# VectorE's order at the end of a stage: additions to the residual, and the rests of the next stage's first two pieces

## The chip, the cores and the metric

The kernel runs on one core of a Trainium2 chip. The core has the engines TensorE (PE, matmuls), VectorE (DVE), ScalarE (ACT), GpSimd (POOL) and SyncE (SP, here only a DMA queue). Each takes its instructions in order; they wait for one another through semaphores. The metric is the device time of one execution in microseconds (us). The kernel before takes 2769.25 us, the median of three runs (2766.05 to 2773.75).

## The reference

A block of two layers and a second block of two layers work on 256 tokens of 1024 channels in float32:

```
# first block, per layer l = 0, 1
h = rmsnorm(x, norm1_g[l]);  x = x + token_mixer(h, w_in[l], ..., w_out[l])      # mix1
h = rmsnorm(x, norm2_g[l])
x = x + swiglu(h, gate, up, down)        # l = 0: ffn1, width 3584
x = x + moe_ffn(h, router, 8 experts)    # l = 1: moe, top 2 of 8, width 3584 each
x = rmsnorm(x, final_g)                                                          # post
# second block, per layer l = 0, 1
x = x + 0.5 * swiglu(rms_norm(x, ffn1_norm), ...)                                # ffn2a, width 2816
x = x + concat(attention, conv) @ w_out  # of rms_norm(x, mix_norm)              # mix2
x = x + 0.5 * swiglu(rms_norm(x, ffn2_norm), ...)                                # ffn2b, width 2816
x = rms_norm(x, post_norm)                                                       # post
```

with `rmsnorm(x, g) = x * rsqrt(mean(x * x) + 1e-6) * g` and `swiglu(h) = (silu(h @ gate) * (h @ up)) @ down`.

## The kernel before

**Stages.** `plan` (line 69) lists the stages in order: mix1, ffn1, mix1, moe, post, and then twice ffn2a, mix2, ffn2b, post. A post stage is only the closing norm. `after(st)` gives the next stage that is no post stage.

**Pieces.** All weights come in pieces of 128 x 2048 float32 (1 MB; a few of mix2 are smaller). SP loads them in order into a ring of six slots, `raw`. To keep the precision of float32, a piece is split in two: ScalarE rounds it into `hi` (`act_hi`, line 439; a ring of three slots), and VectorE subtracts that from the piece, which leaves the rest, `lo` (`lo_piece`, line 1185; it overwrites `raw`). Activations are split in the same way into `xh` and `xl` (in a feed-forward stage's hidden part `hh` and `hl`). Each product is then three matmuls: high by high, high by rest, rest by high. The semaphores `hi_done`, `lo_done` and `multiplied` count pieces. A load into a slot of `raw` waits for `multiplied` of the piece six before, a rounding for that of the piece three before.

**Stage end.** The last four pieces of a mixer and every third of a feed-forward stage multiply into four PSUM banks of 128 x 512, which hold the stage's result for two halves of 128 tokens. For the last piece `pe_last_rows` (lines 737 to 749) does all of the first token half before the second. It raises `first_tile` behind the first half and `multiplied` behind the second. VectorE's `add_down` (line 1252) then adds the four banks to the residual `x` (line 1261), two for each half, and raises `x_done` behind each half. The expert stage (moe) has no `add_down`: it adds within `experts` and then calls `ahead` itself (line 1691).

**Ahead.** The first two pieces of the next stage are split before that stage's norm: ScalarE rounds them in `act_ahead` (line 479), and VectorE makes their rests in `ahead` (line 1222). The second of them is rounded only when the piece before the last is multiplied, since its slot of `hi` is taken until then.

**Norm.** Behind `act_ahead`, ScalarE squares and sums the two halves of `x`, each when `x_done` says so (line 493). VectorE's `norm` (line 1227) makes of each sum a variance (`var`, line 1232), ScalarE takes the root (line 497), and VectorE makes the reciprocal (line 1237) and scales `x` by it and by the gain into `xn` (line 1244; in a post stage into `x`, line 1239). In program order VectorE has both var instructions first, and then reciprocal and scaling for each half. TensorE transposes `xn` into PSUM (line 1071), ScalarE rounds the result into `xh` (line 510), VectorE makes `xl` (line 1249), and the next stage's matmuls begin. POOL loads the gain of a norm when the squares of the norm before it are done (line 1110).

Of the kernel before, what the change touches and what calls it, by code (L numbers as in the profile page):

```python
# [96 lines left out]
def build(nc, A, rope, out):  # L97
    stages = plan()

    with ExitStack() as ctx:  # L100
# [216 lines left out]
        def after(st):  # L317

            return next((n for n in stages[st["Q"] + 1:] if n["kind"] != "post"), None)
# [841 lines left out]
        def _(dve):  # L1161
# [21 lines left out]
            def lo_piece(S, c, i, n=PIECE):  # L1183
                dve.wait_ge(S.hi_done, c + 1 + 6 * i)
                v.tensor_tensor(lo[:, c % RING, 0:n], raw[:, c % RING, 0:n], hi[:, c % HRING, 0:n].bitcast(F32),  # L1185
                                ALU.subtract).then_inc(S.lo_done, 1)
# [35 lines left out]
            def ahead(st):  # L1222

                lo_piece(main, st["B"], 0)
                lo_piece(main, st["B"] + 1, 0)
# [25 lines left out]

            def add_down(st, factor, end):

                if after(st):
                    ahead(after(st))
                dve.wait_ge(first_tile, st["W"] + 1)
                for b in range(4):
                    if b == 2:
                        dve.wait_ge(main.multiplied, end)
                    xs = x[:, b // 2, b % 2 * 512:b % 2 * 512 + 512]  # L1260
                    ins = v.scalar_tensor_tensor(xs, bank[DOWN[b]][:, :], factor, xs, ALU.mult, ALU.add)
                    if b % 2:
                        ins.then_inc(x_done, 1)

            def turned_rest(dst, src, gain, high, signal):

                v.scalar_tensor_tensor(dst, src, gain, high.bitcast(F32), ALU.mult, ALU.subtract).then_inc(signal, 1)  # L1267

            def mix1(st):
# [91 lines left out]
                for k in range(KD):  # L1361
                    dve.wait_ge(ev("yh_out"), 8 * l + bank_end(k, KD))
                    turned_rest(xl[:, k, :], bank[Y_BANKS[k // 2]][:, k % 2 * T:(k % 2 + 1) * T],
                                col(("group", l), k), xh[:, k, :], ev("yl_out"))
                lo_piece(main, B + 11, 0)
                add_down(st, 1.0, B + MIX1_PIECES)

            def router(st):
# [124 lines left out]
            def mix2(st):  # L1493
# [139 lines left out]
                for b in range(2):  # L1633
# [6 lines left out]
                                ALU.subtract).then_inc(ev("catl_out"), 1)  # L1640
                lo_piece(main, B + 13, 0)
                add_down(st, 1.0, B + MIX2_PIECES)

            def constants():
# [27 lines left out]
            for st in stages:  # L1672
                k = st["kind"]
                norm(st)
                if k == "post":
                    continue
                if st["M"] == 0:
                    constants()
                if k == "mix1":
                    mix1(st)  # L1680
                elif k == "mix2":
                    mix2(st)
                elif k == "moe":
                    router(st)
                    experts(main, st, 0)
                    flag = dve.value_load(spill[0:1, 0:1])
                    with dve.If(flag > 0):
                        experts(again, SPILL, 1)
                        dve.nop()
                    dve.end_ifs()  # L1690
                    ahead(after(st))
                    mark(x_done, TT)
                else:
                    ffn(st)
                    add_down(st, 1.0 if k == "ffn1" else 0.5, st["B"] + 3 * st["n"])
# [67 lines left out]
```

## Time and profile before

| | |
|---|---|
| median of three runs | 2769.25 us (2766.05 to 2773.75) |
| profiled execution | 2773.95 us, its span 2771.9 us |
| busy: TensorE, VectorE, ScalarE, POOL | 2482.3, 1796.3, 1381.2, 26.5 us |
| mean granted clock of TensorE | 0.941 of full speed |
| read from HBM | 596.94 MB, 216 GB/s over the span |
| one subtraction of line 1185 | 2.28 us on average, 562 of them |

The profiled execution took 2.05 us around its span. Busy times are sums over a program whose stages differ, so what a change is worth is read where it acts: at the ends of stages. A matmul's start is measured, its end is modelled. In the timelines a merged row gives the start of the first instruction, the busy time of all of them, and in brackets how long the engine sat idle before and what ended that.

### The profile page before, as it was taken

How to read it: one execution, taken by the hardware profiler on the slowest of the kernel's cores; microseconds unless marked ns; L12 is line 12 of the kernel's file. 1: busy time of each engine (PE TensorE's matmuls, PEld its weight loads, DVE VectorE, ACT ScalarE, POOL GpSimd, SP SyncE). 2: the span in 40 equal slices, each digit the busy share in tenths (PEclk: the TensorE clock that was granted, in tenths of full speed). 3: DMA queues.
4: the chain of work that ended last, by engine and by line, in shares of the span. 5: the costliest groups of instructions: out<-in, count | busy, mean ns of one | idle time of the engine just before them, and what ended most of it. 6: DMA issues, size and time to landing. Idle time of an engine off the chain costs nothing.

```text
span 2771.9 us, 42658 instructions
## 1 busy us (share of the span) xinstructions
PE 2482.3 (90%) x16893; PEld 2310.4 (83%) x16893; DVE 1796.3 (65%) x1813; ACT 1381.2 (50%) x1297; POOL 26.5 (1%) x50
## 2 busy tenths in 40 slices
PE   5799987999999999999999799865899899846998
PEld 5699986898989899989989699864799799835897
DVE  5544456588888888787888744559444544486544
ACT  3443334476767666676767544341444433432433
POOL 2000000000000000000000000000000000000000
PEclk9899999799999999999999899985899999976999
DMA  6345543498989898899989645430355455411452
GB/s 222 124 168 189 188 157 131 172 361 310 361 310 360 309 346 323 327 335 331 338 317 354 248 168 186 163 124 1 129 183 187 154 189 182 141 61 46 161 188 98
DMA packets 84816, 599.06 MB, mean 216 GB/s; under 512 B 9812, under 2 KB 10038, under 8 KB 13574
## 3 DMA queue, kind: packets, MB, share of 16 engines
q1 hardware_dynamic: 81216, 587.76, 59.2%
q0 software_dynamic: 3040, 9.13, 1.0%
q8 instruction: 52, 0.85, 0.1%
q10 hardware_dynamic: 486, 1.13, 0.1%
q14 instruction: 22, 0.18, 0.0%
HBM read 596.94 MB, written 1.05 MB: 216 GB/s over the span
## 4 chain that ended last, share of the span: by engine, by line
PE 83%; DVE 12%; ACT 3%; issue 1%; DMA 1%; ACTq 0%; DVEq 0%
PE bank L718 9%; PE bank L720 9%; PE bank L719 9%; PE bank L732 9%; PE bank L733 9%; PE bank L734 9%; PE bank L761 8%; PE bank L763 8%; PE bank L767 8%; DVE lo L1185 3%; DVE acc L1541 3%; ACT hi L439 1%; PE bank L845 1%; PE bank L1071 1%; DMA stage_rows<-in_sgu_b 1%
## 5 line engine op out<-in xcount | busy, mean ns | idle before, releaser
L1185 DVE TENSOR_TENSOR lo<-raw,hi 128x2048 fp32r<-128x2048 f32 (+1 forms) x562 | 1276.9, 2280 | 727.4 <-ACT hi L439 726.3
L439 ACT CAST hi<-raw 128x2048 fp32r<-128x2048 f32 (+1 forms) x562 | 1064.4, 1899 | 642.0 <-PE bank L767 322.1
L732 PE MATMUL bank<-hi,xh 128*128 128x256 f32 (+2 forms) x2088 | 610.0, 292 | 30.4 <-DVE xl L1267 12.8
L733 PE MATMUL bank<-lo,xh 128*128 128x256 f32 (+2 forms) x2088 | 599.0, 287 | 0.0
L734 PE MATMUL bank<-hi,xl 128*128 128x256 f32 (+2 forms) x2088 | 598.7, 287 | 0.0
L718 PE MATMUL bank<-xh,hi 128*128 128x256 f32 x2080 | 591.7, 284 | 7.0 <-DVE xl L1249 7.0
L719 PE MATMUL bank<-xl,hi 128*128 128x256 f32 x2080 | 591.0, 284 | 0.0
L720 PE MATMUL bank<-xh,lo 128*128 128x256 f32 x2080 | 590.9, 284 | 0.0
L732 PEld LDWEIGHTS bank<-hi,xh 128*128 128x128 f32 x2088 | 404.7, 194 | 45.7 <-issue 18.8
L718 PEld LDWEIGHTS bank<-xh,hi 128*128 128x128 f32 x2080 | 401.7, 193 | 11.0 <-DVE xl L1249 8.9
L733 PEld LDWEIGHTS bank<-lo,xh 128*128 128x128 f32 x2088 | 405.5, 194 | 3.2
L734 PEld LDWEIGHTS bank<-hi,xl 128*128 128x128 f32 x2088 | 404.8, 194 | 0.6
L719 PEld LDWEIGHTS bank<-xl,hi 128*128 128x128 f32 x2080 | 401.8, 193 | 2.1
L720 PEld LDWEIGHTS bank<-xh,lo 128*128 128x128 f32 x2080 | 401.6, 193 | 0.0
L761 PE MATMUL bank<-hi,hh 128*128 128x512 f32 x872 | 342.7, 393 | 12.2 <-DVE hl L1202 12.2
L763 PE MATMUL bank<-lo,hh 128*128 128x512 f32 x872 | 342.3, 393 | 0.0
L767 PE MATMUL bank<-hi,hl 128*128 128x512 f32 x872 | 269.7, 390 | 0.0
L446 ACT ACTIVATE sg<-bank 128x256 f32<-128x256 f32 (+1 forms) x170 | 78.2, 460 | 253.3 <-PE bank L720 222.0
L761 PEld LDWEIGHTS bank<-hi,hh 128*128 128x128 f32 x872 | 164.8, 189 | 45.9 <-issue 8.6
L767 PEld LDWEIGHTS bank<-hi,hl 128*128 128x128 f32 x872 | 164.1, 188 | 35.5
L763 PEld LDWEIGHTS bank<-lo,hh 128*128 128x128 f32 x872 | 164.8, 189 | 29.2
L1197 DVE TENSOR_TENSOR hf<-sg,bank 128x256 f32<-128x256 f32 (+1 forms) x170 | 86.2, 507 | 102.6 <-PE bank L720 91.1
(268 smaller groups left out, 1576.9 us busy)
## 6 DMA issues: line engine op xcount, KB each, us to landing
raw<-in_moe_w_gate SPq DMA_DIRECT2D x112, 1024.0 KB, 4.9
raw<-in_moe_w_up SPq DMA_DIRECT2D x112, 1024.0 KB, 4.9
raw<-in_moe_w_down SPq DMA_DIRECT2D x112, 1024.0 KB, 4.9
raw<-in_ffn_w_gate SPq DMA_DIRECT2D x58, 1024.0 KB, 4.9
raw<-in_ffn_w_up SPq DMA_DIRECT2D x58, 1024.0 KB, 4.9
raw<-in_ffn_w_down SPq DMA_DIRECT2D x58, 1024.0 KB, 4.9
raw<-in_mix_pieces SPq DMA_DIRECT2D x46, 1024.0 KB, 4.9
gains<-in_norm_g POOLq DMA_DIRECT2D x4, 512.0 KB, 7.3
```

Source lines behind the costliest of these rows:

```text
L439: nc.scalar.copy(hi[:, c % HRING, 0:n], raw[:, c % RING, 0:n]).then_inc(S.hi_done, 1)
L718: pe.matmul(o, hi[:, hr, a:a + P], xh[:, k, 0:w], start=(k == 0), stop=False)
L719: pe.matmul(o, hi[:, hr, a:a + P], xl[:, k, 0:w], start=False, stop=False)
L720: mm = pe.matmul(o, lo[:, r, a:a + P], xh[:, k, 0:w], start=False, stop=(k == KD - 1))
L732: pe.matmul(o, xh[:, x0 + k, tk], hi[:, hr, wgt], start=(first and n == 0), stop=False)
L733: pe.matmul(o, xh[:, x0 + k, tk], lo[:, r, wgt], start=False, stop=False)
L734: mm = pe.matmul(o, xl[:, x0 + k, tk], hi[:, hr, wgt], start=False, stop=(last and n == len(ks) - 1))
L761: pe.matmul(o, ah[:, s, tk], hi[:, hr, wgt], start=(first and s == 0), stop=False, skip_group_check=True)
L763: pe.matmul(o, ah[:, s, tk], lo[:, r, wgt], start=False, stop=False, skip_group_check=True)
L767: mm = pe.matmul(o, al[:, s, tk], hi[:, hr, wgt], start=False, stop=(last and s == 1), skip_group_check=True)
L1185: v.tensor_tensor(lo[:, c % RING, 0:n], raw[:, c % RING, 0:n], hi[:, c % HRING, 0:n].bitcast(F32), ALU.subtract).then_inc(S.lo_done, 1)
L1197: v.tensor_tensor(o, a, b, ALU.mult).then_inc(S.hf_done, 1)
```

## The change

In `add_down` the two lines that call `ahead` move from the front to the end. VectorE makes the four additions first and the rests of the next stage's first two pieces behind them. Nothing else differs. At the end of the last stage `after(st)` is empty and the function is as before.

```diff
             def add_down(st, factor, end):
 
-                if after(st):
-                    ahead(after(st))
                 dve.wait_ge(first_tile, st["W"] + 1)
                 for b in range(4):
                     if b == 2:
                         dve.wait_ge(main.multiplied, end)
                     xs = x[:, b // 2, b % 2 * 512:b % 2 * 512 + 512]
                     ins = v.scalar_tensor_tensor(xs, bank[DOWN[b]][:, :], factor, xs, ALU.mult, ALU.add)
                     if b % 2:
                         ins.then_inc(x_done, 1)
+                if after(st):
+                    ahead(after(st))
```

## Rows read from the trace of the kernel before

**Rows 1.** Page, part 4: the chain that ended last, by engine.

```profile
PE 83%; DVE 12%; ACT 3%; issue 1%; DMA 1%; ACTq 0%; DVEq 0%
```

**Rows 2.** Waits of SP's queue, whole trace: us in total, times, longest.

```profile
SPq L356 <- PE bank L747: 46.8, 8, 6.8
```

**Rows 3.** Line 1261, the additions: count and duration in ns.

```profile
L1261 DVE SCALAR_TENSOR_TENSOR x<-bank,x x36: 677/680/692, 125.4 to 2763.9; 128x512 f32<-128x512 f32 x36
```

**Rows 4.** Chain of waits, end of ffn1: start us, us, what.

```profile
372.57 4.49 DVE lo L1185 x2
377.06 2.40 DVE x L1261 x4
...
381.03 0.76 DVE xn L1244
```

**Rows 5.** DVE's timeline, end of ffn1: start us, us, instruction [idle before].

```profile
376.99 2.47 DVE L1261 SCALAR_TENSOR_TENSOR x<-bank,x 128x512 f32<-128x512 f32 x4
```

**Rows 6.** DVE's timeline, end of the first mixer.

```profile
117.75 2.29 DVE L1185 TENSOR_TENSOR lo<-raw,hi 128x2048 fp32r<-128x2048 f32 x1 [3.15 <-ACT hi L439]
...
125.40 2.52 DVE L1261 SCALAR_TENSOR_TENSOR x<-bank,x 128x512 f32<-128x512 f32 x4
...
129.50 1.42 DVE L1244 SCALAR_TENSOR_TENSOR xn<-x,rstd,gains 128x512 f32<-128x512 f32 x2
```

**Rows 7.** DVE's timeline, the last stage, which has none after it.

```profile
2760.60 1.29 DVE L1261 SCALAR_TENSOR_TENSOR x<-bank,x 128x512 f32<-128x512 f32 x2 [3.11 <-PE bank L747]
2763.32 1.29 DVE L1261 SCALAR_TENSOR_TENSOR x<-bank,x 128x512 f32<-128x512 f32 x2 [1.43 <-PE bank L747]
2764.52 0.14 DVE L1232 TENSOR_SCALAR var<-ssq 128x1 f32<-128x1 f32 x1
2765.82 0.15 DVE L1232 TENSOR_SCALAR var<-ssq 128x1 f32<-128x1 f32 x1 [1.15 <-ACT xn L493]
```

**Rows 8.** PE's timeline, end of ffn1: last piece, transposes.

```profile
371.52 0.73 PE L747 MATMUL bank<-hi,hh 128*128 128x512 f32 x2 [1.43 <-DVE hl L1202]
...
381.84 3.67 PE L1071 MATMUL bank<-ident,xn 128*128 128x128 f32 x16 [4.59 <-DVE xn L1244]
```

**Rows 9.** PE's timeline, end of the first mixer: last piece, transposes.

```profile
121.00 0.61 PE L747 MATMUL bank<-hi,xh 128*128 128x512 f32 x2
...
130.30 1.32 PE L1071 MATMUL bank<-ident,xn 128*128 128x128 f32 x8 [3.71 <-DVE xn L1244]
```

**Rows 10.** PE's timeline, the last stage: last piece's first matmuls.

```profile
2757.55 0.73 PE L747 MATMUL bank<-hi,hh 128*128 128x512 f32 x2 [1.43 <-DVE hl L1202]
```

**Rows 11.** DVE's timeline inside a mixer: a root fetched from ScalarE.

```profile
1939.94 0.17 DVE L1626 TENSOR_SCALAR var<-bna 128x2 f32<-128x2 f32 x1
1940.38 0.17 DVE L1628 RECIPROCAL rstd<-std 128x2 f32<-128x2 f32 x1 [0.27 <-ACT std L649]
1940.58 1.53 DVE L1630 TENSOR_SCALAR xn<-bank,bna,rstd 128x512 f32<-128x512 f32 x2
```

**Rows 12.** Windows, PE, the 6 us after a seam: busy, PEclk, DMA.

```profile
485.10:491.10 6.00, 6.00 (x36) 0.63 0.01 3
1589.80:1595.80 6.00, 6.00 (x28) 0.50 0.00 0
1791.70:1797.70 6.00, 6.00 (x50) 1.00 0.00 0
...
2183.50:2189.50 6.00, 5.97 (x39) 0.75 0.00 0
```

**Rows 13.** Waits, all engines: the only one of a conversion on weights.

```profile
ACT hi L439 <- DMA raw<-in_mix_pieces: 4.9, 2, 3.7
```

**Rows 14.** POOL's timeline at the seam with a closing norm.

```profile
2173.29 0.53 POOL L1110 DMA_DIRECT2D gains<-in_ffn_norm  x1 [198.69 <-ACT xn L493]
```

**Rows 15.** Tile gains at that seam: landing times.

```profile
DMA to landing us min/median/max: 3.9/3.9/3.9
```

**Rows 16.** Chain of waits at that seam.

```profile
2177.64 0.76 DVE xn L1244
```

## The prediction

> **What bounds the kernel now.** I read first the shares of the chain that ended last: TensorE has 83% of it and VectorE 12% [rows 1]. So the kernel is bound by matmuls, with stretches between stages in which VectorE sets the time. Then I looked for transfers, because a time bound by them could swallow a delay. There are none: SP's queue stands waiting for TensorE to release a slot, at each of the 8 last pieces that have a stage after them too [rows 2], and of all conversions of weights only two waited for a transfer, 4.9 us together [rows 13].
>
> The additions of line 1261 are 36, four for each of nine stages [rows 3]. One of the nine, the last, has no stage after it. So the change acts at 8 places, which I call seams: four end a feed-forward stage (ffn1, ffn2a twice, the first ffn2b), four end a mixer. The expert stage makes its two rests by a path of its own and is not touched.
>
> The chain at a seam shows that the two rests (lo) and the four additions stand on the path one behind the other, and that behind them come the squares, the root and the scaling that feeds the transposes [rows 4]. At a mixer's end only the second rest stands in front of the additions; the first was made 7.6 us earlier in idle time of VectorE [rows 6].
>
> **The change, part by part.** It adds and removes no instruction, transfer or semaphore. Per seam two 128x2048 subtractions move from before the four additions to behind them, and so ahead of the two var instructions, the reciprocals and the scaling of the next norm, which VectorE takes in order.
>
> *What it takes off.* The last stage is a feed-forward stage without these rests and shows when the additions can start. Its last piece starts on TensorE at 2757.55 [rows 10], the first pair of additions starts at 2760.60 (3.05 later), the second at 2763.32 (5.77), and the next instruction runs at 2764.52 (6.97) [rows 7]. At ffn1's end the piece starts at 371.52 [rows 8] and the additions run from 376.99 for 2.47 us, to 7.94 after it [rows 5]. So the additions end 0.97 us earlier. At the mixer's end the piece starts at 121.00 [rows 9]. Its first pair of matmuls took 0.61 us against 0.73 [rows 8, 9], so I take 0.12 off: the additions would end 6.85 after it, where they end now at 125.40 + 2.52 = 127.92, or 6.92 [rows 6]. There the gain is 0.07, since TensorE's last matmul, not the rest, all but sets their end already.
>
> *What it puts on.* The two rests take 376.99 - 372.57 = 4.42 us, from the first's start to the additions' [rows 4, 5]. Behind the additions the squares of the second half run on ScalarE anyway; the wait for them covers part of this. In the last stage the var instruction that needs them starts at 2765.82, or 8.27 after the piece's start [rows 7, 10]. The rests end at 6.97 + 4.42 = 11.39 (mixer 11.27). So the squares are hidden and the rests are what is late. Then the root has to be fetched from ScalarE: now the first half's root is ready while the second half's squares run, in the changed kernel both var instructions come only behind the rests. The same fetch inside a mixer takes 1940.58 - 1939.94 = 0.64 us from var to the first use [rows 11].
>
> *The sum per seam*, as the start of the scaling (xn) after the last piece's start:
> - feed-forward: now 381.03 - 371.52 = 9.51 [rows 4, 8]; then 11.39 + 0.64 = 12.03; later by 2.52.
> - mixer: now 129.50 - 121.00 = 8.50 [rows 6, 9]; then 11.27 + 0.64 = 11.91; later by 3.41.
>
> Four of each: 10.1 + 13.6 = 23.7 us. From the scaling on, transposes, rounding and the first matmuls are the same instructions, so all of it moves. What lies ready is the rest that the next stage's first matmul wants: it ends 0.64 us ahead of the scaling.
>
> *Queues that the step is moved past.* ScalarE waits for VectorE meanwhile and its two roundings of weights are ahead of the squares as before. SP's queue waits for TensorE alone. POOL loads a gain when the squares are done. At the seam with a closing norm this is close now: issued at 2173.29, 3.9 us to land, first used at 2177.64 [rows 14 to 16], a slack of 0.45. Afterwards the use is 2.5 us later and the squares end no later. Now the issue goes out beside the closing norm's first reciprocal, 4.35 before the use. In the changed kernel that reciprocal comes 0.44 behind the rests' end (1940.38 - 1939.94 [rows 11]) and the use some 4.35 behind it, 4.8 in all. So even if the issue could not go out beside VectorE's rests and waited for their end, it would land 3.9 after it, in time. I take 0; the bounds are 0 and 0.5.
>
> *The clock of TensorE.* Its idle time before the transposes, now 4.59 (feed-forward) and 3.71 (mixer) [rows 8, 9], becomes about 7.1 at both (4.59 + 2.52, 3.71 + 3.41). In the 6 us after a seam's first matmul the granted clock is not the same at all of them: at three of the eight it is 1.00 (the first at 1791.7), at five between 0.63 (485.1) and 0.75 (2183.5) [rows 12]. With two levels, 2.4 and 1.2 GHz, the time lost in 6 us is 6 x (1 - clock): 0 at three, about 1.9 at five, 9.4 in all. The longer idle time cannot be read from any seam exactly; the nearest ones are the eight themselves, with gaps of 3.7 and 4.6, and the expert stage's seam, idle far longer, with 0.50, or 3.0 lost [rows 12]. I take half of what the three full-clock seams could lose, 3 x 1.9 / 2 = +3. Bounds: -9.4, all seams at full clock, and 8 x 3.0 - 9.4 = +14.6.
>
> The Trainium skill's page "TensorE: Matmul & The Clock Gate", section "Part 1: The HAM clock gate (the "warmup" mystery)", says that an idle TensorE falls to half clock and gets the full one back only after sustained activity. The trace agrees in part: by that rule no seam with this much idle time should find the full clock at its first matmuls, and three do, their transposes having run just before. Its result is the second rival.
>
> Together 23.7 + 3 = 26.7 us. Set on the profiled execution's 2773.95 this is 2800.7. That execution is 4.7 us above the median of the three runs, 2769.25; the difference applies to either, and a median is what will be compared, so 2769.25 + 26.7 = 2796.
>
> **The rivals.**
> 1. *Every seam starts at the low clock.* The three seams at 1.00 lose as the five do: 3 x 1.9 = 5.7, or 2.4 to 3.0 at each if they behave as the expert stage's. For it: the idle time grows by 2.5 to 3.4 us. Against it: the idle time is not all that decides, since both clocks are found behind today's gaps. 23.7 + 5.7 to 14.6, some 33 us: 2802.
> 2. *The clock falls out kindly.* The delayed starts land so that more seams find the full clock; the five lose half: -4.7, so +19: 2788.
> 3. *Not slower: transfers are the bound behind the seams and catch up.* If a stage later waits for its weights, 3 us of delay at its start let the transfers run ahead and the wait shrinks by the same amount. This decides from the point where such waits sum to the 23.7 us put on. Against it: 4.9 us of them in the whole trace, and a ring of pieces that is full, so that SP can't run ahead [rows 2, 13]. With all absorbed and the 0.97 of four seams kept it would be 2769 - 4 = 2765.
> 4. *The change does less than it says*: the rests are hidden in the wait for squares wholly. Then the additions' earlier end would remain. It would need rests of 8.27 - 6.97 = 1.30 us, a third of what is measured; I give it no more than a trace of chance, with rival 3.
>
> **How the numbers follow.** Forecast (24 to 30 us more) 0.62, rival 1 0.20, rival 2 0.14, rivals 3 and 4 0.04. The predicted time is the forecast's, 2796. The range goes from 2785 (+16, most of rival 2) to 2806 (+37, rival 1 with its longer low stretches). Runs of the kernel before lie between 2766.05 and 2773.75, which the ends allow for too. About 0.3%, 8 us, can be told from no change. Faster 0.01, same 0.03, slower 0.96: only rivals 3 and 4, or a very kind clock, stay below 8 us.
>
> **What would show it.** In the profile of the changed kernel: the first pair of additions waits for TensorE, 3.05 us (feed-forward) or 2.9 (mixer) after its last piece's start; the second pair starts 2.7 later; directly behind it the two rests with no idle time, and then two var instructions side by side; the scaling starts 12.0 and 11.9 after the last piece's start; TensorE's idle time before the transposes is near 7.1 at seven seams and longer only at the one with a closing norm. I am wrong if a rest is found before the additions, if the scaling shifts by other amounts, if SP's waits for TensorE vanish behind a seam, or if the sum of the eight shifts is right but the time is not: then it is the clock term.

## The result and the profile after

The changed kernel took 2789.9 us, the median of three runs (2789.6 to 2791.34), against 2769.25: 20.65 us more, a ratio of 1.0075 (95% interval 1.0055 to 1.0095). Five more rounds gave 1.0087 (1.0073 to 1.0100). Its profiled execution took 2789.6 us, its span 2787.6.

The chain by engine is nearly the same as [rows 1]:

```profile
PE 84%; DVE 12%; ACT 2%; issue 1%; DMA 1%; ACTq 0%; DVEq 0%
```

VectorE's timeline at ffn1's end, the answer to [rows 4, 5] (start us, us, instruction, idle time before):

```profile
373.06 1.29 DVE L1259 SCALAR_TENSOR_TENSOR x<-bank,x 128x512 f32<-128x512 f32 x2 [3.11 <-PE bank L747]
375.77 1.29 DVE L1259 SCALAR_TENSOR_TENSOR x<-bank,x 128x512 f32<-128x512 f32 x2 [1.43 <-PE bank L747]
376.98 4.48 DVE L1185 TENSOR_TENSOR lo<-raw,hi 128x2048 fp32r<-128x2048 f32 x2
381.38 0.20 DVE L1232 TENSOR_SCALAR var<-ssq 128x1 f32<-128x1 f32 x2
381.86 0.16 DVE L1237 RECIPROCAL rstd<-std 128x1 f32<-128x1 f32 x1 [0.28 <-ACT std L497]
382.06 1.42 DVE L1244 SCALAR_TENSOR_TENSOR xn<-x,rstd,gains 128x512 f32<-128x512 f32 x2
```

The additions now wait for TensorE in two pairs, and behind them the two rests run without a gap. The last piece started at 370.00, so the scaling at 382.06 is 12.06 behind it; it was 9.51, and 12.03 was forecast. The two var instructions stand side by side behind the rests, and the reciprocal waits 0.28 for the root: var to scaling is 0.68, forecast 0.64.

The same at the first mixer's end, for [rows 6]:

```profile
120.28 1.29 DVE L1259 SCALAR_TENSOR_TENSOR x<-bank,x 128x512 f32<-128x512 f32 x2 [9.31 <-PE bank L747]
123.00 1.29 DVE L1259 SCALAR_TENSOR_TENSOR x<-bank,x 128x512 f32<-128x512 f32 x2 [1.43 <-PE bank L747]
124.20 4.48 DVE L1185 TENSOR_TENSOR lo<-raw,hi 128x2048 fp32r<-128x2048 f32 x2
128.60 0.21 DVE L1232 TENSOR_SCALAR var<-ssq 128x1 f32<-128x1 f32 x2
129.08 0.16 DVE L1237 RECIPROCAL rstd<-std 128x1 f32<-128x1 f32 x1 [0.28 <-ACT std L497]
129.28 1.42 DVE L1244 SCALAR_TENSOR_TENSOR xn<-x,rstd,gains 128x512 f32<-128x512 f32 x2
```

The last piece started at 117.36, so the scaling comes 11.92 behind it (11.91 forecast; before 8.50). In the idle 9.31 us ahead of the first pair VectorE has nothing to do: there the first rest stood before.

TensorE's timeline, transposes at both seams, for [rows 8, 9]:

```profile
382.87 3.54 PE L1071 MATMUL bank<-ident,xn 128*128 128x128 f32 x16 [7.13 <-DVE xn L1244]
```

```profile
130.09 2.18 PE L1071 MATMUL bank<-ident,xn 128*128 128x128 f32 x9 [7.13 <-DVE xn L1244]
```

The idle time is 7.13 at either, where 7.1 was forecast. Over all eight seams the scaling comes later by 2.55, 2.55, 2.55 and 2.54 (feed-forward) and 3.42, 3.43, 3.42 and 3.41 (mixers), 23.87 us together.

At the seam with a closing norm POOL's gain is no bound. POOL's timeline, for [rows 14], and VectorE's, for [rows 16]:

```profile
2181.00 0.53 POOL L1110 DMA_DIRECT2D gains<-in_ffn_norm  x1 [201.31 <-ACT xn L493]
```

```profile
2179.44 4.48 DVE L1185 TENSOR_TENSOR lo<-raw,hi 128x2048 fp32r<-128x2048 f32 x2
2183.84 0.20 DVE L1232 TENSOR_SCALAR var<-ssq 128x1 f32<-128x1 f32 x2
2184.33 0.16 DVE L1237 RECIPROCAL rstd<-std 128x1 f32<-128x1 f32 x1 [0.28 <-ACT std L497]
2184.52 1.28 DVE L1239 SCALAR_TENSOR_TENSOR x<-x,rstd,gains 128x1024 f32<-128x1024 f32 x1
2185.73 0.16 DVE L1237 RECIPROCAL rstd<-std 128x1 f32<-128x1 f32 x1
2185.92 1.28 DVE L1239 SCALAR_TENSOR_TENSOR x<-x,rstd,gains 128x1024 f32<-128x1024 f32 x1
2187.12 0.15 DVE L1232 TENSOR_SCALAR var<-ssq 128x1 f32<-128x1 f32 x1
2188.42 0.15 DVE L1232 TENSOR_SCALAR var<-ssq 128x1 f32<-128x1 f32 x1 [1.15 <-ACT xn L493]
2188.58 0.16 DVE L1237 RECIPROCAL rstd<-std 128x1 f32<-128x1 f32 x1
2188.78 1.42 DVE L1244 SCALAR_TENSOR_TENSOR xn<-x,rstd,gains 128x512 f32<-128x512 f32 x2
```

The load went out at 2181.00, in the middle of the two rests, and the loads of this stretch landed within 3.9 to 4.1 us: by 2185.1, with 3.7 us to the use at 2188.78. VectorE's rests did not hold it up.

TensorE alone, 6 us from each seam's first matmul (busy, granted clock, DMA), the answer to [rows 12]:

```profile
135.10:141.10 6.00, 5.98 (x49) 1.00 0.01 3
387.80:393.80 6.00, 5.99 (x50) 1.00 0.01 3
489.20:495.20 6.00, 6.00 (x29) 0.50 0.01 3
...
2194.70:2200.70 6.00, 6.00 (x36) 0.67 0.00 0
```

Six of eight seams are at 1.00 (the other four not shown too), one at 0.67 and one at 0.50. By the prediction's own formula, 6 x (1 - clock), 5.0 us are lost there, against 9.4 before. The spans of the two profiled executions differ by 2787.6 - 2771.9 = 15.7 us, in this way: 23.9 at the seams; 0.2 from scaling to first matmul; -3.6 before the first seam is reached, where no instruction differs (clock over that stretch 0.96 against 0.93); -4.8 in the eight stretches between a seam's first matmul and the next seam, of which the clock behind the seams is -4.4. The two traces thus hold 23.9 us of order and about 8 us of clock the other way, of which 3.6 cannot come from the change; only medians of more runs tell how much of the clock stays.

Nor does the trace of one execution show that the change made the seams behind it warmer. The first mixer's end is the test: up to it the kernel before and e8 (below) run the same instructions, and TensorE is idle for 3.71 us before its transposes in both. Yet the 6 us behind it were at 0.72 in the one and at 1.00 in the other:

```profile
135.20:141.20 6.00, 6.00 (x38) 0.72 0.01 3
```

```profile
131.40:137.40 6.00, 6.00 (x50) 1.00 0.01 3
```

So the clock at a seam differs between executions without any difference in the program. Nor does the length of the gap sort the profiles. Leaving out the seam with a closing norm, where the gap is longer in every kernel, e8's gaps are 3.71, e2's 3.71 or 7.14 and the changed kernel's 7.13, and each has six of eight seams at 1.00; e3's are 4.59 or 7.14, and it has two.

### The profile page after: what moved, and what is told of

It reads as the page before. It is cut to its first block, busy times and chain, and to the rows that moved or that the text cites. A ratio compares the mean times of both kernels' runs of the same rounds, so it can differ in the third digit from the quotient of the medians.

```text
span 2787.6 us, 42658 instructions
## 1 busy us (share of the span) xinstructions
PE 2474.1 (89%) x16893; PEld 2304.3 (83%) x16893; DVE 1794.8 (64%) x1813; ACT 1381.1 (50%) x1297; POOL 26.2 (1%) x50
## 4 chain that ended last, share of the span: by engine, by line
PE 84%; DVE 12%; ACT 2%; issue 1%; DMA 1%; ACTq 0%; DVEq 0%
PE bank L718 9%; PE bank L720 9%; PE bank L719 9%; PE bank L732 9%; PE bank L733 9%; PE bank L734 9%; PE bank L761 8%; PE bank L763 8%; PE bank L767 8%; DVE lo L1185 3%; DVE acc L1541 3%; PE bank L747 2%; PE bank L1071 1%; PE bank L845 1%; DMA stage_rows<-in_sgu_b 1%
```

## The experiments

All ratios are to the kernel before on the same chip, of which 10 to 29 runs were made beside them.

| run | median us | ratio (95%) | seams, us |
|---|---|---|---|
| e1 changed kernel again | 2794.11 | 1.0087 (1.0073 to 1.0100) | +23.9 |
| e2 feed-forward ends only | 2778.0 | 1.0030 (1.0019 to 1.0041) | +10.2 |
| e3 mixers' ends only | 2784.24 | 1.0048 (1.0034 to 1.0061) | +13.7 |
| e4 one rest behind | 2782.81 | 1.0048 (1.0034 to 1.0062) | +6.3 |
| e5 before, filled | 2763.84 | 0.9980 (0.9971 to 0.9989) | 0 |
| e6 changed, filled | 2788.32 | 1.0069 (1.0053 to 1.0085) | +23.9 |
| e7 one rest behind, filled | 2770.95 | 1.0011 (1.0001 to 1.0021) | +6.3 |
| e8 second rest late | 2766.4 | 0.9986 (0.9976 to 0.9996) | -3.5 |
| e9 before, filled in two places | 2757.7 | 0.9967 (0.9954 to 0.9979) | 0 |
| e10 changed, filled in two places | 2787.17 | 1.0067 (1.0053 to 1.0081) | +23.9 |
| e11 second rest late, filled in two places | 2757.23 | 0.9963 (0.9949 to 0.9977) | -3.5 |

The kernel before: 2767.89 beside e1 to e4, 2768.25 beside e5 to e8, 2768.28 beside e9 to e11. The last column is the sum over the eight seams of what the trace shows from the last piece's start to the scaling, less the same before.

**e1.** The changed kernel, unaltered.

> The changed kernel once more, in five rounds, for a narrower interval. Theory A (the two rests lie wholly on the path, less what the squares and the earlier additions hide): 4 x 2.55 + 4 x 3.42 = +23.9 us, a ratio of 1.0086, and the clock adds nothing on average. Theory B (the stages behind the seams catch up a part, by transfers that ran ahead or by a kinder clock): the 20.65 us of the three rounds hold, or less, at 1.0055 to 1.0075, with stages between the seams shorter by about 1 us each. Theory C (the longer idle time costs clock): 27 to 33 us, 1.0098 to 1.012.

26.2 us by the medians, 24 by the ratio. Theory A's 1.0086 is in the middle of the interval; B's highest value, 1.0075, and C's lowest, 1.0098, lie just within its edges.

**e2 and e3.** In `add_down`, e2 (e3 with the two kinds exchanged):

```diff
-                if after(st):
+                if after(st) and st["kind"][:3] == "mix":
                     ahead(after(st))
 ...
+                if after(st) and st["kind"][:3] == "ffn":
+                    ahead(after(st))
```

> The rests behind the additions only at the four ends of feed-forward stages; mixers' ends as before. Theory A: scaling 2.55 us later at these four and 0 at the others, +10.2 us, 1.0037. Theory B with a fixed share caught up: 8.8 us or less. A rival that puts the cost into one price per seam, whatever its kind: half of the whole, +11.9.

> The rests behind the additions only at the four ends of mixers. Theory A: 3.42 us later at each, +13.7 us, 1.0049, so more than at the feed-forward ends, because before there the first rest was made in idle time. One price per seam: +11.9, the same as with the feed-forward ends. The two halves should add up to the whole.

By the ratios +8.3 and +13.3 us. The traces settle it seam by seam: in e2 the feed-forward ends moved by 2.54 to 2.55 and the mixers' by 0.01 at most, in e3 the mixers' by 3.42 to 3.44 and the feed-forward ends by 0.01. One price per seam is refuted, and the whole is the sum of its halves (21.6 against 24.1 by the ratios, within their intervals).

**e4.** One rest on either side:

```diff
                 if after(st):
-                    ahead(after(st))
+                    lo_piece(main, after(st)["B"], 0)
 ...
+                if after(st):
+                    lo_piece(main, after(st)["B"] + 1, 0)
```

> At all eight seams the first rest stays ahead of the additions, the second goes behind them. Theory A: feed-forward end, the additions end at 6.97 after the last piece's start and the one rest at 9.18, then 0.64 to the scaling, 9.82 against 9.51, +0.3; mixer's end 6.85 + 2.21 + 0.64 = 9.70 against 8.50, +1.2; in all 4 x 0.3 + 4 x 1.2 = +6 us, 1.0022, a quarter of the whole and not half, since the squares hide the first 1.3 us behind the additions. A rival in which each rest costs its own duration at each seam: half of 23.9, +12.

A miss, and the most useful one. VectorE's timeline at its first mixer's end:

```profile
120.97 1.29 DVE L1261 SCALAR_TENSOR_TENSOR x<-bank,x 128x512 f32<-128x512 f32 x2 [3.87 <-PE bank L747]
123.69 1.29 DVE L1261 SCALAR_TENSOR_TENSOR x<-bank,x 128x512 f32<-128x512 f32 x2 [1.43 <-PE bank L747]
124.89 2.28 DVE L1185 TENSOR_TENSOR lo<-raw,hi 128x2048 fp32r<-128x2048 f32 x1
127.09 0.21 DVE L1232 TENSOR_SCALAR var<-ssq 128x1 f32<-128x1 f32 x2
127.58 0.17 DVE L1237 RECIPROCAL rstd<-std 128x1 f32<-128x1 f32 x1 [0.28 <-ACT std L497]
127.78 1.41 DVE L1244 SCALAR_TENSOR_TENSOR xn<-x,rstd,gains 128x512 f32<-128x512 f32 x2
```

The seams did what was expected: 127.78 is 9.73 behind the last piece's start at 118.05, later by 1.23, and the feed-forward ends by 0.35, in all 6.3 us. Yet the kernel is 13 us slower by the ratio, with 9.4 us the lower end of the interval. The clock behind its seams:

```profile
133.70:139.70 6.00, 6.00 (x35) 0.66 0.01 3
386.10:392.10 6.00, 6.00 (x34) 0.64 0.01 3
485.60:491.60 6.00, 5.97 (x29) 0.50 0.01 3
...
1983.70:1989.70 6.00, 5.98 (x35) 0.66 0.00 0
2189.40:2195.40 6.00, 5.96 (x38) 0.73 0.00 0
```

All eight seams are below full clock (the three not shown at 0.68, 0.71 and 0.66), with 16.6 us lost by the same formula against 9.4: 7.2 more, and 6.3 + 7.2 = 13.5. That this meets the measured 13 is in part luck: the spans of the two profiled executions it is read from differ by only 9.3, since 2.9 us came back before the first seam. All five runs of e4 have a low mean clock, 0.938 to 0.941, against a median of 0.943 for the kernel before, which points to the clock too. The changed kernel, with 7.1 us of idle time before its transposes, had six seams at full clock; this one, with 4.9, has none. So longer idle time doesn't by itself mean a colder start.

**e5, e6 and e7.** TensorE is kept busy through the seam; in `pe_last_rows`, behind the last matmul (15, 19 and 37 in e5; 30 and 48 in e6; 20 and 38 in e7):

```diff
+        def keep_busy(pe, n):
+            for _ in range(n):
+                pe.matmul(bank[0][:, :], zeros[:, 0:P], zeros[:, :], start=True, stop=True, skip_group_check=True)
 ...
                 mm.then_inc(first_tile if t == 0 else main.multiplied, 1)
+            nxt = next((st for st in stages if st["B"] == c + 1), None)
+            if nxt is not None and nxt["Q"] < len(stages) - 1:
+                keep_busy(pe, 37 if nxt["kind"] == "post" else 19 if nxt["Q"] in (2, 6, 10) else 15)
```

> The kernel before, with TensorE kept busy through the eight seams: behind the last piece it multiplies zeros into a free bank, 15 matmuls of 128x512 at a mixer's end, 19 at a feed-forward end, 37 where a closing norm follows, each some 0.23 us at full clock, so that they end before the first transpose. The clock at the seams should then be 1.00 at all eight, and the 9.4 us that the profile of before lost there in the first 6 us go: about -8 us, 0.997. If the clock is not what the spare time goes to, 0 +-1. It is the base for the next two, from which the clock is taken out.

> The changed kernel with the same filling, 30 matmuls at seven seams and 48 at the one with a closing norm. Theory A (the rests are on the path, the clock of a seam is a term of its own): +23.9 us against the filled kernel before (e5), whatever the two do against the unfilled ones; against the kernel before +23.9 - 8 = +16. Rival (a part of the measured 20 to 26 us is clock): e6 less e5 is clearly below 23, by the part that is clock.

> One rest ahead and one behind (as e4, which came out at +13 us where its seams account for +6.3), with the filling, 20 matmuls at seven seams and 38 at the closing norm. If the 7 us left over in e4 were the clock (its first 6 us behind the seams lost 16.6 us against 9.4), e7 less e5 is +6.3 us. If they are a cost of the order itself, e7 less e5 is still about +13.

e5 gained 4.4 us by the medians and 5.5 by the ratio, where 8 was expected, which is the edge of the interval. The clock was not full at all seams:

```profile
380.60:386.60 6.00, 5.99 (x37) 0.72 0.00 0
479.40:485.40 6.00, 6.00 (x36) 0.65 0.00 0
...
2170.20:2176.20 6.00, 5.99 (x37) 0.72 0.00 0
```

Five are at 1.00, three still at 0.65 to 0.72. A part of the gain lies ahead of these windows: from the scaling to the first matmul the eight seams take 43.3 us together in e5, against 46.6 before, the transposes being faster. What the filled kernels are for is the difference: e6 less e5 is 24.5 us (0.0089), as theory A has it and not clearly below 23; the intervals leave some 5 us on it. e7 less e5 is 7.1 us by the medians and 8.6 by the ratios (4.9 to 12.3), near 6.3 and away from 13. Since the two have the same order as e4 and the kernel before, this points to the clock for the greater part of e4's extra 7 us; it is not shown, as the interval overlaps e4's own (9.4 to 17), and the filling did not take the clock out: the profile of e6 had seven seams at 1.00, that of e7 only three. A single execution can be far from the median here, e6's profiled one by 10 us (2778.63) and e7's by 6.6 the other way (2777.54). The filled profiles keep the seams' shifts to 0.02 us.

**e8.** A version meant to be faster than the kernel before: at feed-forward ends only the first rest stays ahead, and the second goes behind the next norm's `xl`.

```diff
                 if after(st):
-                    ahead(after(st))
+                    lo_piece(main, after(st)["B"], 0)
+                    if st["kind"][:3] == "mix":
+                        lo_piece(main, after(st)["B"] + 1, 0)
+                    else:
+                        late.append(after(st)["B"] + 1)
 ...
                                         ALU.subtract).then_inc(xl_done, 1)
+                    if late:
+                        lo_piece(main, late.pop(), 0)
```

> A candidate without filling: at the four feed-forward ends the first rest stays ahead of the additions and the second goes behind the next norm's xl, where the matmuls of the first piece (about 6 us) cover it; mixers' ends as before. The additions should end at 6.97 instead of 7.94, the second half's var run at 8.27 instead of 9.15 and the scaling start at 8.63 instead of 9.51: 4 x -0.88 = -3.5 us of seams, ratio 0.9987. The clock can move this by some us either way: it lost between 5.0 and 16.6 us at the seams of the kernels so far. So a result between -8 and +8 us is expected of it, and only the seams in the trace will show the -0.88.

VectorE's timeline at its ffn1's end:

```profile
369.53 1.28 DVE L1269 SCALAR_TENSOR_TENSOR x<-bank,x 128x512 f32<-128x512 f32 x2
372.04 1.29 DVE L1269 SCALAR_TENSOR_TENSOR x<-bank,x 128x512 f32<-128x512 f32 x2 [1.23 <-PE bank L747]
373.24 0.14 DVE L1232 TENSOR_SCALAR var<-ssq 128x1 f32<-128x1 f32 x1
374.54 0.15 DVE L1232 TENSOR_SCALAR var<-ssq 128x1 f32<-128x1 f32 x1 [1.16 <-ACT xn L493]
374.70 0.16 DVE L1237 RECIPROCAL rstd<-std 128x1 f32<-128x1 f32 x1
374.90 1.41 DVE L1244 SCALAR_TENSOR_TENSOR xn<-x,rstd,gains 128x512 f32<-128x512 f32 x2
...
380.51 2.28 DVE L1185 TENSOR_TENSOR lo<-raw,hi 128x2048 fp32r<-128x2048 f32 x1
```

The scaling starts 8.64 behind the last piece (366.26), 0.87 earlier than before; the late rest at 380.51 is covered. The ratio, 0.9986, is -3.9 us (the medians differ by 1.9), and its interval excludes 1 narrowly.

**e9, e10 and e11.** As e5, e6 and (with e8's order) a filled e8, and five more matmuls of zeros behind the transposes of every stage but the first:

```diff
                 if st["M"] == 0:
                     pe_constants(pe)
+                else:
+                    keep_busy(pe, 5)
```

> As e5, with five more matmuls of zeros between the transposes and the stage's first matmul, an idle time of 1.4 to 1.7 us in which e5 still started three of its eight seams at 0.65 to 0.72. If that idle time is what keeps the clock low there, all eight are at 1.00 and the time falls by a further 5.5 us against e5, to about 2758; if not, it stays at e5's 2764.

> The changed kernel with the filling of e6 and the five more matmuls. With the seams' clock at 1.00 in both, e10 less e9 is the price of the order alone: theory A +23.9 us. If the longer idle time had cost clock in the unfilled kernels by itself, the difference would now be smaller than the 26 us of e1 and the 24.5 of e6 less e5, by more than 3 us.

> The candidate of e8 (second rest behind xl at feed-forward ends, -3.5 us of seams) with the filling, 15 matmuls at seven seams and 33 at the closing norm, and the five more. Additive: e9's time less 3.5, about 2754 us, ratio 0.995. If the two gains shared one cause (the same idle time), no better than the better one of e8 and e9.

Now the clock holds at seven of eight seams in the profiles of e9, e10 and e11; windows of e10, the first three:

```profile
138.20:144.20 6.00, 5.96 (x49) 1.00 0.00 0
390.60:396.60 6.00, 6.00 (x50) 1.00 0.00 0
491.50:497.50 6.00, 6.00 (x37) 0.66 0.01 3
```

The exception is the seam before the router, at 0.66 here and 0.77 in e9; why was not looked into. e9 is 10.6 us faster than before by the medians, 9.1 by the ratio. That is 6.1 more than e5 by the medians and 3.6 by the ratios, whose intervals overlap. It suggests that at two of e5's three cold seams the short idle time behind the transposes kept the clock low; with one profile of each, and seven seams at 1.00 in e6 without the five matmuls, it is not shown. e10 less e9 is 29.5 us by the medians and 0.0100, or 27.7 us, by the ratios, with intervals wide enough for 23.9 (some 5 us on the difference). The difference did not shrink when the clock was held, which speaks against the rival that the longer idle time itself costs clock. It doesn't exclude a small cost: by the ratios e1's 24 us are 3.6 below e10 less e9, with some 6 us on that, so up to 3 us of clock remain possible. The two profiles differ by 27.1 us: 23.9 at the seams, 2.7 before the first seam, 0.5 elsewhere. The 2.7 are no effect of the order, since no edit of e10 acts before that seam; over all the profiles of this case the last piece there starts anywhere from 116.9 to 121.0. e11, expected at 2754, came to 2757.23, 11 us below before but not distinguishable from e9. It is the fastest version by its ratio; e8's and e9's gains are not shown to add.

## Why the prediction was right

- *The rests are late behind the additions, the squares are not.* Right: at all eight seams the scaling moved by the forecast amount to within 0.03 us, which leaves no room for another wait at the seams. The two rests took 381.38 - 376.98 = 4.40 us, forecast 4.42.
- *The sizes.* 2.52 and 3.41 forecast, 2.55 and 3.42 measured; 23.7 forecast in all, 23.87 measured. The 0.03 is mostly the root's fetch (0.68 for 0.64). Why it is longer is open: the second var is not the reason, as it ends at 381.58 and the reciprocal starts 0.28 behind it.
- *Additions end 0.97 and 0.07 earlier.* At ffn1's end the rests start at 376.98, 6.98 behind the last piece (6.97 forecast); at the mixer's 6.84 (6.85).
- *Feed-forward against mixers.* e2 and e3 separate them as forecast. The dearer seams are those where the moved rest had idle time of its own.
- *POOL and SP.* Both right: the gain had 3.7 us to spare, and the ring was full. SP's waits for TensorE at the eight last pieces are what they were in [rows 2]:

```profile
SPq L356 <- PE bank L747: 46.8, 8, 6.8
```

- *The clock, +3 us.* This is the weak term. Its central value assumed that longer idle time leaves the seams as cold or colder. It also took the gaps of the eight seams as 3.7 and 4.6, and missed the one with a closing norm, which was idle for 8.85 us before and, at 0.75, no colder than the others:

```profile
2178.45 0.90 PE L1071 MATMUL bank<-ident,xn 128*128 128x128 f32 x3 [8.85 <-DVE xn L1244]
```

  The profile of the changed kernel lost 4.4 us less there, e4 with a shorter idle time 7.2 us more. The medians put the clock's net part at -3 (20.65 less 23.9) and, over five rounds, at +2: by size it was nothing that these runs tell from zero. The bounds of -9.4 to +14.6 held. Rival 1, all seams cold, describes e4 and not the changed kernel; rival 2, a kind clock, describes the changed kernel's profile, and the first three rounds came out 6 us below the forecast, in its direction. What decides the clock at a single seam was not settled: the same instructions and the same gap gave 0.72 and 1.00.
- *Transfers catching up* was given almost nothing, and nothing of it was seen: the stretches between seams that got shorter did so with the clock.

The term that was off in size is thus the clock alone: of the 6 us between the forecast shift, 26.7, and the first measured one, 20.65, it holds 3, and the rest is clock and spread on the measured side (the changed kernel's runs lie between 2789.5 and 2795.23). The first three rounds lie below the forecast's own 24 to 30 us; the five of e1, 24 to 26, lie within it. How close the total comes is therefore no test of the +3: the order's 23.7 carried the prediction. That e10 less e9 is some 4 us above 23.9 stays open; the intervals allow chance.

## What to carry to other kernels

Work for the next stage belongs where the in-order engine idles anyway, or behind the last link of the chain (e8), and never between the additions and the norm that waits for them: each microsecond there, less what the squares hide, is paid in full at every seam. Such a shift can be forecast to 0.05 us from the rows of the seam and of one stage without the moved work; the clock of TensorE behind an idle stretch could not, and it moves a run by as much as an effect of a few microseconds. Such an effect is read from the seams, and the total asks for many runs.

## What the runs showed of the hardware

The length of the idle time did not by itself set the clock behind it. The same instructions with the same 3.71 us of idle time were followed by 0.72 in one execution (before) and by 1.00 in another (e8). One profiled execution each had three seams at 1.00 (before), two (e3), none (e4) and six (changed, e2, e8).

With multiplications of zeros both ahead of and behind the transposes, all three profiles had 1.00 at seven of eight seams (e9, e10, e11), and the kernel before became shorter by 9 to 11 us (ratio 0.9967). With the filling ahead alone it was five, seven and three seams (e5, e6, e7). That the idle time of 1.4 to 1.7 us between transposes and first matmul takes part is thus suggested, not shown.
